# A per-row ScalarE chain for the gathered expert rows, and its TensorE sum one position earlier

## The reference, cut to what matters

```
def step(args):
    tc, ec, gc = args
    hid = jax.nn.gelu(jnp.einsum('td,thkd->thk', tc, u[ec]), approximate=False)
    return jnp.einsum('thk,thkd->td', gc * hid, v[ec])
```

## Time and profile before

| what | value |
|---|---|
| times of three executions | 2165.26, 2167.34, 2168.16 us (median 2167.34) |
| span of the profiled execution | 2168.7 us |
| TensorE / VectorE / ScalarE / GpSimd busy | 1855.1 / 1305.5 / 493.1 / 687.5 us |
| bytes moved | 781.44 MB, of which the gathers 542.37 MB |
| mean granted TensorE clock | 0.955 |

### The profile page before, as it was taken

One profiled execution on the slowest core, in us unless ns is written; L12 is line 12 of the kernel. 1 busy time (PEld: TensorE's weight loads), 2 busy tenths in 40 slices (PEclk: granted clock), 3 DMA queues, 4 the chain that ended last, 5 costly groups with the idle time before them and its releaser, 6 DMA issues.

```text
span 2168.7 us, 19290 instructions
## 1 busy us (share of the span) xinstructions
PE 1855.1 (86%) x5992; PEld 893.5 (41%) x5992; DVE 1305.5 (60%) x3327; ACT 493.1 (23%) x1232; POOL 687.5 (32%) x593
## 2 busy tenths in 40 slices
PE   9999999998799989999877787777888767878875
PEld 4445555333245445455433333333433433434332
DVE  1343433221033668667587797987777898777764
ACT  1232221111022233222221122222212222222221
POOL 2110001111000334344343344453434444444442
PEclk9999999999999999999998998889999988999999
DMA  7432367999795999999999999999999999999996
GB/s 250 168 122 81 128 271 249 415 418 419 293 385 201 395 390 374 422 420 421 421 422 421 420 399 415 422 416 421 421 421 421 392 409 416 422 421 421 421 410 259
DMA packets 115081, 781.44 MB, mean 360 GB/s; under 512 B 16080, under 2 KB 17792, under 8 KB 21664
## 3 DMA queue, kind: packets, MB, share of 16 engines
q0 software_dynamic: 78928, 542.37, 60.9%
q1 hardware_dynamic: 32544, 227.75, 26.4%
q10 hardware_dynamic: 3504, 10.04, 1.2%
HBM read 782.20 MB, written 10.49 MB: 366 GB/s over the span
## 4 chain that ended last, share of the span: by engine, by line
DMA 29%; DVE 17%; issue 14%; POOL 6%; PE 5%; ACT 0%; POOLq 0%; DVEq 0%; ACTq 0%
DMA arena<-in_c_rows_dram,arena 29%; DVE arena L2716 7%; POOL arena L2818 6%; PE banks L1824 2%; DVE x L2726 2%; PE banks L2702 1%; DVE arena L2610 1%; DVE arena L2613 1%; DVE arena L2619 1%; PE banks L1915 1%; DVE arena L2648 1%; DVE arena L2652 0%; DVE arena L2577 0%; DVE small L2607 0%; DVE xn L417 0%
## 5 line engine op out<-in xcount | busy, mean ns | idle before, releaser
L2702 PE MATMUL banks<-arena 128*128 128x512 f32 x1784 | 885.4, 642 | 240.0 <-ACT arena L2783 239.1
L2818 POOL DMA_INDIRECT arena<-in_c_rows_dram,arena x512 | 609.7, 1191 | 817.5 <-PE banks L2702 571.3
L2716 DVE CUSTOM_DVE_ANT_0 arena<-arena,xn 128x1024 f32<-128x1024 f32 x512 | 625.4, 1223 | 296.9 <-DMA arena<-in_c_rows_dram,arena 294.2
L2702 PEld LDWEIGHTS banks<-arena 128*128 128x128 f32 x1784 | 345.8, 203 | 714.2 <-issue 356.6
L2783 ACT ACTIVATE arena<-ident,small 128x128 f32<-128x128 f32 x446 | 158.2, 395 | 536.6 <-DVE small L2723 524.7
L314 PE MATMUL banks<-ring,hT 128*128 128x512 f32 (+1 forms) x480 | 202.2, 577 | 0.0
L376 ACT COPY arena<-banks 128x512 f32<-128x512 f32 (+4 forms) x218 | 101.2, 493 | 292.5 <-PE banks L360 112.7
L2774 ACT ACTIVATE small<-small 128x2 f32<-128x2 f32 x256 | 52.1, 204 | 499.1 <-DVE small L2716 498.9
L402 POOL TENSOR_TENSOR small<-small 128x1 f32<-128x1 f32 (+4 forms) x24 | 33.5, 1398 | 303.3 <-DVE small L398 276.9
L314 PEld LDWEIGHTS banks<-ring,hT 128*128 128x128 f32 x480 | 87.9, 191 | 100.1 <-issue 98.4
L2407 PE MATMUL banks<-ring,hT 128*128 128x512 f32 x176 | 88.3, 606 | 0.0
(11 more groups left out here) (319 smaller groups left out, 1805.3 us busy)
## 6 DMA issues: line engine op xcount, KB each, us to landing
arena<-in_c_experts_dram SPq DMA_DIRECT2D x51, 1024.0 KB, 21.5
ring<-in_c_w_in_dram SPq DMA_DIRECT2D x30, 1024.0 KB, 4.8
ring<-in_c_experts_dram SPq DMA_DIRECT2D x30, 1024.0 KB, 24.9
ring<-in_c_odd_w_in_dram SPq DMA_DIRECT2D x19, 1024.0 KB, 9.8
ring<-in_c_w_q_dram SPq DMA_DIRECT2D x18, 1024.0 KB, 9.6
ring<-in_c_even_w_in_dram SPq DMA_DIRECT2D x12, 1024.0 KB, 19.2
arena<-in_c_even_w_in_dram SPq DMA_DIRECT2D x10, 1024.0 KB, 15.4
arena<-in_c_rows_dram,arena POOLq DMA_INDIRECT x512
```

Of the source, the lines that this page charges most:

```text
L2702: r = e.matmul(banks[:, bank_of[("acc", L, c, hf)], :], diag[:, diag_of[m], :], rows[:, row_of[m], D + hf * 512:D + (hf + 1) * 512], start ...
L2716: e.tensor_tensor_reduce(u, u, xn[:, c, :], 1.0, 0.0, ALU.mult, ALU.add, hid3[:, c, h, k:k + 1]).then_inc(ve.sem, ve.up(("u", p)))
L2818: e.indirect_dma_start(rows[:, b, :], None, table_uv, bass.IndirectOffsetOnAxis(ap=eix[:, c, 16 * h + k:16 * h + k + 1], axis=0)).then_inc ...
```

## The change

The gelu, the gate and the diagonal of a row stop being done for pairs. ScalarE does gelu (L2768 after), the product with the gate (L2771, formerly on VectorE) and the diagonal (L2777) for each row at the row's own position. TensorE sums row p-1 at position p. Where a row is on VectorE, the addition stands at the next position and waits for ScalarE's product.

```diff
         def pe_position(e, p):
             for what in beside.get(p, ()):
                 pe_beside(e, what)
-            if p % 2 and p >= 3:
-                for m in (p - 3, p - 2):
-                    if m < LAST and not on_dve(m):
-                        pe_value(e, m)
+            if 1 <= p <= LAST and not on_dve(p - 1):
+                pe_value(e, p - 1)
...
-            if p % 2 == 0 and 0 <= p - 2 < LAST:
-                L, c, h, k = SLOTS[p - 2]
-                hv = hid3[:, c, h, k:k + 2]
-                e.wait_ge(ve.sem, ve.at(("gate", L, c, h)))
-                e.wait_ge(ac.sem, ac.at(("gelu", p - 2)))
-                e.tensor_tensor(hv, hv, top3[:, c, h, k:k + 2], ALU.mult).then_inc(ve.sem, ve.up(("w", p - 2)))
-                if on_dve(p - 1):
-                    e.wait_ge(ve.sem, ve.n)
-                    e.scalar_tensor_tensor(x[:, c, :], rows[:, row_of[p - 1], D:2 * D], hid3[:, c, h, k + 1:k + 2],
-                                           x[:, c, :], ALU.mult, ALU.add).then_inc(ve.sem, ve.up(("v", p - 1)))
+            if 1 <= p <= LAST and on_dve(p - 1):
+                L, c, h, k = SLOTS[p - 1]
+                e.wait_ge(ac.sem, ac.at(("w", p - 1)))
+                chain(e, ve)
+                e.scalar_tensor_tensor(x[:, c, :], rows[:, row_of[p - 1], D:2 * D], hid3[:, c, h, k:k + 1],
+                                       x[:, c, :], ALU.mult, ALU.add).then_inc(ve.sem, ve.up(("v", p - 1)))
...
         def act_position(e, p):
-            if p % 2 and p < LAST:
-                L, c, h, k = SLOTS[p - 1]
-                hv = hid3[:, c, h, k:k + 2]
+            if p < LAST:
+                L, c, h, k = SLOTS[p]
+                hv = hid3[:, c, h, k:k + 1]
                 e.wait_ge(ve.sem, ve.at(("u", p)))
-                e.activation(hv, hv, ACT.Gelu).then_inc(ac.sem, ac.up(("gelu", p - 1)))
-            if p % 2 == 0 and 0 <= p - 2 < LAST:
-                e.wait_ge(ve.sem, ve.at(("w", p - 2)))
-                for m in (p - 2, p - 1):
-                    if not on_dve(m):
-                        L, c, h, k = SLOTS[m]
-                        e_before = diag_before[m]
-                        if e_before is not None:
-                            e.wait_ge(pe.sem, pe.at(("v", e_before)))
-                        e.activation(diag[:, diag_of[m], :], ident[:, :], ACT.Copy,
-                                     scale=hid3[:, c, h, k:k + 1]).then_inc(ac.sem, ac.up(("diag", m)))
+                e.activation(hv, hv, ACT.Gelu).then_inc(ac.sem, ac.up(("gelu", p)))
+                e.wait_ge(ve.sem, ve.at(("gate", L, c, h)))
+                e.wait_ge(ac.sem, ac.at(("gelu", p)))
+                e.activation(hv, hv, ACT.Copy, scale=top3[:, c, h, k:k + 1]).then_inc(ac.sem, ac.up(("w", p)))
+                if not on_dve(p):
+                    e_before = diag_before[p]
+                    if e_before is not None:
+                        e.wait_ge(pe.sem, pe.at(("v", e_before)))
+                    e.wait_ge(ac.sem, ac.at(("w", p)))
+                    e.activation(diag[:, diag_of[p], :], ident[:, :], ACT.Copy,
+                                 scale=hv).then_inc(ac.sem, ac.up(("diag", p)))
```

## The result

The changed kernel takes 2155.22 us in the median of four runs (2152.86 to 2157.04), against 2167.56 us (2165.26 to 2168.16) for the kernel before. The medians lie 12.3 us apart; the ratio of the runs is 0.9947, with a 95% interval of 0.9933 to 0.9961. A later repetition of the changed kernel gave 2156.35 us (2151.41 to 2158.86, ratio 0.9943, interval 0.9927 to 0.996). The profiled execution has a span of 2155.2 us, 13.5 less than that of before.

What follows compares the result with a forecast made beforehand. The prediction took the full DMA engines to bound the kernel from 870 us on. Gains of 5.5 + 3 + 1.5 = 10.0 us from the median 2167.34 gave 2157.3 us, range 2147 to 2167.

Steps and rivals of the forecast that it cites:

- The first stretch: 720 to 870 us: shorter TensorE waits for diagonals close part of the DMA gaps; 5.5 us, between 0 and 8.3.
- A buffer free 4.1 us earlier, 1.6 rows more in stock: Steady stretch: dot to gather falls from 8.6 to 4.5 us, so the DMA engines hold 1.6 rows more.
- Later windows: 1240 to 2080 us without 1700 to 1720: deeper stock covers short stalls; 3 us, bounds 0 and 7.9.
- the load in 1240 to 1300 us: VectorE loses its products; in this window some 11 pairs or 1.7 us, elsewhere worth nothing.
- The norm near 1700: 1700 to 1720 us: GpSimd stands before the norm's rsqrt, gathers can't pass it; the 3.4 us lacking stay.
- ScalarE: Its 256 more gelus and 512 gates, 0.20 us each, 154 us in all, cost nothing while ahead of their readers.
- The end: Row 510's diagonal follows its own dot, so VectorE's collection stops waiting for TensorE; 1.5 us, between 1.0 and 1.64.
- The lagging engine: Rival: the slowest DMA engine has no pause in the gaps, so only the end gains; 2165.8 us, chance 0.21.
- Everything closes: Rival: TensorE keeps up through 720 to 870 us, all gaps close, 22 us go; 2145.3 us, chance 0.17.
- A higher rate: Rival: the DMA rate itself rises with the stock, one per cent giving some 12 us more; 2145 us, chance 0.02.
- VectorE waits for ScalarE: Slower rival: the middle segments' 64 additions wait for ScalarE's gate, up to 19 us; 2176 to 2185 us, chance 0.10.

Runs made afterwards that it cites:

- e6: Changed kernel with TensorE summing per row up to position 56 and in pairs from there on: 2155.60 us, ratio 0.9947.
- e1: Changed kernel with TensorE summing rows in pairs again throughout, ScalarE's chain still per row: 2160.54 us, ratio 0.9963.
- e5: Changed kernel with TensorE summing in pairs up to row 55 and per row behind: 2163.53 us, ratio 0.9981.
- e10: Kernel before with only TensorE's sums moved, rows p-2 and p-1 at even positions, ScalarE and VectorE still in pairs: 2184.84 us, ratio 1.0082.
- e2: Changed kernel with seven row buffers throughout instead of nine from position 53 on: 2156.41 us, ratio 0.9944.
- e7: Changed kernel with 256 unused products put back on VectorE, which wait for nothing of ScalarE: 2155.04 us, ratio 0.9943.
- e3: Changed kernel with gathers allowed 7 positions ahead of a norm's rsqrt instead of 5: 2155.45 us, ratio 0.9937.
- e4: Changed kernel with two more unused 128x1 ScalarE copies behind each diagonal, 892 in all: 2155.96 us, ratio 0.994.
- e9: Changed kernel with the sum of row p-1 ahead of TensorE's other work of position p: 2159.33 us, ratio 0.9964.

## Why the prediction was right

It gave 2157.3 us; 2155.2 came, 2.1 us less.

*The first stretch, taken 5.5.* Right in place and size: 5.2 us to the 29th dot, and from 720 to 870 us a lack of (421 - 404) / 421 x 150 = 6.1 us instead of 12.5. The source was only half right, so the close size is partly luck. The term was to come from the 8.3 us in which TensorE's sums wait for a diagonal; from 720 to 870 us these fell by 1.6 us only, to 6.7. The stretch from the first dot to the 29th, before and after, with the columns of the earlier trace rows, shows more:

```profile
716.90:808.00 91.10, 84.44 (x255) 42.35 (x253) 63.30 (x177) 26.40 (x61) 32.02 (x28) 0.96 0.97 392
712.90:798.80 85.90, 84.68 (x263) 42.53 (x262) 62.19 (x164) 38.41 (x105) 34.11 (x29) 1.00 1.01 420
```

TensorE's idle time falls from 6.7 to 1.2 us. Its waits for diagonals go from 3.0 us to none, but its waits for ScalarE's unloading of the scores (L2346), which the prediction left standing, also go from 3.7 to 1.2. e6 has it with the new order for the first 56 rows alone, e1 and e5 lose it. What it rests on is both parts together: e10 moved the sums without the diagonals and lost 17.8 us. In the prediction the diagonal's own place was a term of the chain; it is a condition of this gain.

*A buffer free 4.1 us earlier, 1.6 rows more in stock.* The size was right (4.66 against 4.5 us from dot to gather). In the steady stretch it comes from ScalarE's order alone, since e1 and e6 have it with the sums in pairs. What it is worth past the first stretch was wrong: e2 takes two buffers away, which is more than the 1.6 rows, and the times don't show it.

*Later windows, taken 3 from a deeper stock.* 3.3 us came between the 29th dot and the last (-0.2 + 2.2 + 1.3), so the size was right by luck and the reason wrong. e1 and e5 have these 3.3 us as well with the old order on TensorE in the first stretch or throughout. They belong to the other half of the edit: gate on ScalarE, no product on VectorE. e7 gives back 1.7 of them at most, the pure load. The 1.7 us that the prediction gave the load in 1240 to 1300 us were not seen: at the 261st dot e7 leads the kernel before by 6.0 us, the changed kernel's two profiles by 5.6 and 6.8 (all with the first dot's start taken off). VectorE's wait for a pair's gelu is gone, 9.3 us in five places, but the trace of the kernel before puts these elsewhere: 1.1 us at 835.76, three from 900 to 1100 us, and 0.3 at the very end.

```profile
DVE small L2723 <- ACT small L2774: 7.9, 3, 3.8
```

None lies near 1700 us or at the step to the 511th dot, where most of the gain came. So its cause stays open; the runs show only that it goes with ScalarE's chain by rows and without VectorE's product, which were not tried apart.

*The norm near 1700, left as it was.* GpSimd stands there as forecast, a little longer (7.62 us), and its mechanism is the one that was named, since e3 removes it with two positions of `AHEAD`. But no 3.4 us lie there to be had by closing the dip: e3 closes it and gains nothing. The 1.9 us that did come beside this norm, from the 321st to the 351st dot, were not forecast for it.

*ScalarE, costed at nothing.* Right: the additions waited 0.7 us for it, and e4 laid 208 us more on it unharmed. The gate was mis-sized, 0.20 against 0.29; in the chain it is the 0.1 us that was missing, on the path of the last row alone. The Trainium skill names the price, on the page "ScalarE: Activation LUTs", section What ACT_TABLE_LOAD costs: every operand that is a pointer to a 128x1 adds some 93 ns to an activation. The runs agree: 294 ns for the gate, whose scale is such an operand, 202 for the gelu and 203 for e4's copy, whose scales are constants. The Trainium skill's advice on the page "Perfetto Trace Analysis", section Optimizing Scalar/DVE Operations, that larger operations can help, speaks of a saturated engine; ScalarE is busy for 33% of the span here. The other half of that section, to break up what makes bubbles elsewhere, agrees with e1, where only ScalarE's chain by rows and the missing product on VectorE are left of the edit, and which is still 8.5 us under the kernel before.

*The end, taken 1.5.* The table's "behind" fell by 1.0 in this profile (15.6 to 14.6), and by 1.4 (to 14.2) in six of the other kernels with ScalarE's chain by rows. What differs is TensorE's clock. In e6_pairs_late the last sum ran at 1.98 us, and the collection followed the addition of row 511 at once, as the prediction had it:

```profile
2140.07 1.98 PE L2705 MATMUL banks<-arena 128*128 128x512 f32 x4 [2.88 <-ACT arena L2782]
...
2142.09 1.28 DVE L2725 SCALAR_TENSOR_TENSOR x<-arena,small,x 128x1024 f32<-128x1024 f32 x1 [0.66 <-ACT small L2776]
2143.48 1.41 DVE L2747 TENSOR_TENSOR x<-x,banks 128x512 f32<-128x512 f32 x2
```

In the changed kernel's profile it took 3.78 us at 1.2 GHz and ended behind the addition. The clock can take back 0.4 us of the step. It also had a share in the 1.64 us that the prediction put down to the gate alone: in the profile of the kernel before the granted clock was 0.63 and 0.51 in 2152 to 2156 us. e10_pairs_next has the same order at the end with a granted clock of 1.00, and its collection waits 1.19 us:

```profile
2172.07 1.41 DVE L2748 TENSOR_TENSOR x<-x,banks 128x512 f32<-128x512 f32 x2 [1.19 <-PE banks L2702]
```

So the step is right, but at the full clock on both sides it is worth 15.2 - 14.2 = 1.0 us; the term of 1.5 counted some 0.45 us of clock.

*The lagging engine, a rival at 0.21.* It is half true. Below is the tail of the gathers in the changed kernel:

```profile
2128.00:2130.00 2.00, 1.84 (x4) 0.68 (x4) 1.23 (x2) 0.51 (x3) 0.00 (x0) 1.00 0.90 373
...
2138.00:2140.00 2.00, 0.00 (x0) 0.00 (x0) 1.81 (x3) 0.50 (x2) 0.00 (x0) 0.94 0.06 25
2140.00:2142.00 2.00, 1.52 (x2) 0.84 (x3) 1.85 (x3) 0.52 (x2) 0.00 (x0) 0.50 0.00 0
```

A share of 0.06 is one engine of 16. It works for some 7 us behind the others, where before it was about 5. In e2_seven the share falls below one half only at 2134 and is 0.04 at 2138 to 2140: with less stock the others can't run so far ahead of it. That would be how a lower mean rate costs nothing (e2, e3), and why a window's lack against 421 GB/s was a price in the first stretch and not behind it. That the others run ahead of this engine is what the traces show; that the rows land at its pace is argued from it, and no run tried it. As a forecast of the time (2165.8) the rival fell; by its own argument the first stretch must then have been a gap of that engine too. *Everything closes*: refuted as a time (2145.3). Up to the 29th dot all did close, at 420 GB/s and with TensorE busy for 84.7 of 85.9 us; from 720 to 870 us as a whole it did not, with TensorE busy for 140.8 of 150 us. *A higher rate*: refuted, the long windows stay at 417 to 421 GB/s. *VectorE waits for ScalarE*: refuted by 0.7 us.

*What the sum doesn't have.* 5.2 + 3.3 + 1.0 = 9.5 us lie behind the first dot, and 12.3 were timed. The other 2 to 3 us fit the earlier start of the first dot (by 2.2 to 4.0 in the two profiles), which lies ahead of all changed work. The prediction had nothing for it. That part stays open, as does what makes the one DMA engine late. So of the 10.0 us in the sum, some 5 came from where they were sought, 1.0 of the end's 1.5 is the step that was named, and the agreement of the rest is luck.

## What to carry to other kernels

Before the last reader of a buffer is moved ahead of other work on its engine, what feeds it must be moved too, on every engine of the chain: moving only TensorE's sums cost 17.8 us, moving the diagonals with them gained 12.3, and moving the sums ahead of all other work of their position (e9) gained nothing more. Where nothing stands between the sums, their order is worth nothing (e6). A profile that places the gain is worth more than a total of waits, since the 9.3 us of waits that went away lay where nothing was gained. Buffers freed earlier pay only where the stock of transfers runs out; count how long the transfers queue (17.7 us here, seven rows) before paying for more of it. And read the pace by a mark that both traces share, such as the start of the n-th dot, because the mean share of the DMA engines can fall without loss when one of them is the slowest.

## What the runs showed of the hardware that was not expected

- On ScalarE a 128x1 activation with a scale from memory takes 294 ns, with a constant one 203 ns.
- TensorE stood idle for 2.9 to 3.2 us ahead of its last sum in the kernels with ScalarE's chain by rows, and the four matmuls then took anything from 1.98 us (e1, e6) to 3.78 us (the changed kernel twice and e3): the lower clock (granted 0.50) came in some executions and not in others behind nearly the same wait. Behind 2.2 us of idleness the last sums of the kernel before, eight matmuls, took 5.40 us, and the first four of them in e10 1.98.
- In the same kernel family one DMA engine finishes the gathers some 3.5 us (7 buffers) to 7 us (9 buffers) behind the other fifteen; in e4 about two do.
- Stretches whose code is the same in all versions differ by 1.7 us between 10 and 46 us of the span from one version to the next, and two profiles of one version agree to 0.3 us there (44.12 and 44.43).
